# A hybrid attention and MLP layer on one core: latent token tiles loaded already turned, with the next tile's scaling put directly behind the queries' scaling

## What is computed

```python
def modulate(x, g, shift, scale):
    return rmsnorm(x, g) * (1.0 + scale) + shift

h_lat = modulate(x, g_attn[i], sh1, sc1)        # (1024, 1024)
h_ctx = modulate(ctx, g_attn[i], csh1, csc1)    # (256, 1024)
z = h @ w_in                                    # 1184 columns: cq, ckv, kr, qs, ks, vs
q_m = rmsnorm(rmsnorm(cq, g_q_a) @ w_uq)        # keys and values alike from ckv @ w_ukv
```

## Time and profile before

| | us |
|---|---|
| median of three executions | 1398.95 |
| the profiled execution's own time | 1399.78 |
| its span, first to last instruction | 1398.0 |
| token stage, steps 0 and 1 with the start, up to PE's `project(2, 0)` | 58.4 |
| step 2 | 25.8 |
| steps 3 to 8, each | 20.3 |
| step 9 and the last finishing, up to the first scores | 24.8 |
| attention, output projection and MLP | 1167 |

### The profile page before, as it was taken

The page is one execution under the profiler, slowest core; times in us unless marked ns, Lnnn a source line. Parts: engine busy times, 40 slices in busy tenths (PEclk is TensorE's granted clock), DMA queues, the critical chain, the costliest instruction groups (busy, mean ns, idle before and its releaser), DMA issues.

```text
span 1398.0 us, 18825 instructions
## 1 busy us (share of the span) xinstructions
PE 1357.5 (97%) x7262; PEld 1149.4 (82%) x7262; DVE 914.6 (65%) x1284; ACT 692.6 (50%) x1343; POOL 487.1 (35%) x321
## 2 busy tenths in 40 slices
PE   5899997999999999999999999999999999999999
PEld 1688987999899988988887888888888888888887
DVE  1878776777777877875774646547564654746463
ACT  2755655788778777972223424333332433333240
POOL 2766553121299992501102303132050323205010
PEclk8999998999999999999999999999999999999999
DMA  9555658433365646301123112121211212121013
GB/s 377 192 162 160 177 159 286 129 89 86 115 199 144 190 131 191 71 1 61 31 76 121 31 31 90 31 75 31 62 44 30 91 31 75 30 62 44 15 61 121
DMA packets 121576, 143.42 MB, mean 103 GB/s; under 512 B 8184, under 2 KB 103288, under 8 KB 118672
## 3 DMA queue, kind: packets, MB, share of 16 engines
q1 hardware_dynamic: 121232, 142.18, 32.6%
q0 software_dynamic: 256, 0.05, 0.0%
HBM read 108.38 MB, written 31.74 MB: 100 GB/s over the span
## 4 chain that ended last, share of the span: by engine, by line
PE 70%; DVE 11%; POOL 7%; ACT 6%; DMA 4%; issue 1%; SPq 1%; DVEq 0%; ACTq 0%; POOLq 0%
PE f_ps L2062 24%; PE f_ps L2331 19%; PE o_ps L1770 6%; PE a_ps L1422 4%; PE a_ps L1438 3%; PE f_ps L2347 3%; POOL l_wg L1349 3%; ACT s_pr L1519 3%; POOL l_gate L1351 3%; PE t_ps L956 2%; PE a_ps L1468 2%; DVE s_nmx L1604 2%; PE t_ps L945 1%; DMA t_wm<-in_w_mod 1%; DMA l_v<-scratch_v 1%
## 5 line engine op out<-in xcount | busy, mean ns | idle before, releaser
L2062 PE MATMUL f_ps<-h,f_w 128*128 128x512 f32 x1536 | 358.0, 389 | 0.4 <-DVE h L1836 0.2
L2062 PEld LDWEIGHTS f_ps<-h,f_w 128*128 128x128 f32 x1536 | 288.1, 188 | 60.7 <-DVE h L1836 0.7
L2261 DVE TENSOR_TENSOR mix<-mix,f_ps 128x512 f32<-128x512 f32 x196 | 128.7, 683 | 152.9 <-PE f_ps L2331 152.9
L2102 POOL TENSOR_TENSOR f_w<-f_w,f_g 128x1024 f32<-128x1024 f32 x30 | 77.0, 2590 | 390.2 <-DMA f_w<-in_w_mlp 342.7
L2139 ACT ACTIVATE f_a<-f_ps 128x512 f32<-128x512 f32 x64 | 38.2, 597 | 254.7 <-PE f_ps L2062 254.7
L2331 PE MATMUL f_ps<-f_bh,f_al 128*128 128x512 f32 x392 | 152.5, 389 | 0.0
L2331 PE MATMUL f_ps<-f_bh,f_ah 128*128 128x512 f32 x392 | 152.5, 389 | 0.0
L2331 PE MATMUL f_ps<-f_bl,f_ah 128*128 128x512 f32 x392 | 152.5, 389 | 0.0
L1618 DVE TENSOR_TENSOR l_pT<-a_ps,l_pT 128x512 fp32r<-128x512 f32 (+1 forms) x192 | 108.9, 594 | 54.0 <-ACT l_pT L1529 53.9
L1422 PE MATMUL a_ps<-l_k,l_q 96*128 96x512 f32 (+1 forms) x576 | 136.5, 366 | 1.6 <-DMA l_v<-scratch_v 1.1
L956 PE MATMUL t_ps<-w_in,t_h 128*128 128x416 f32 (+2 forms) x600 | 125.7, 355 | 0.3 <-DVE w_in L719 0.3
(11 more groups left out here) (223 smaller groups left out, 2425.1 us busy)
## 6 DMA issues: line engine op xcount, KB each, us to landing
l_wg<-in_w_mod SPq DMA_DIRECT2D x8, 2048.0 KB, 8.0
f_w1r<-in_w_mlp SPq DMA_DIRECT2D x32, 512.0 KB, 4.0
f_w<-in_w_mlp SPq DMA_DIRECT2D x16, 1024.0 KB, 5.0
t_wm<-in_w_mod SPq DMA_DIRECT2D x8, 1024.0 KB, 12.5
scratch_k<-t_kT SPq DMA_DIRECT2D x20, 384.0 KB, 3.7
l_k<-scratch_k SPq DMA_DIRECT2D x8, 960.0 KB, 10.6
scratch_q<-t_qT SPq DMA_DIRECT2D x16, 384.0 KB, 3.9
l_q<-scratch_q SPq DMA_DIRECT2D x8, 768.0 KB, 6.3
```

Source lines behind the costliest of these rows:

```text
L2062: last = nc.tensor.matmul(ps[:, b, :], w1[:, g % 2, w, k, :], h2[x][:, k, half * HB:(half + 1) * HB], start=(k == 0 and i == 0), stop=(k = ...
L2261: V.tensor_tensor(x, x, ps[:, bank_of(i, t), :].rearrange("p (k c) -> p k c", c=P), ALU.add).then_inc(added, 1)
```

## The change

- The host lays out the latent tokens a second time, turned: `x_cols`, per tile 128 rows of the model's width on the partitions, 8 times 128 tokens. SP loads these into `xT` (`load_xT`, 512 KB a tile); the untouched `x` is still loaded for the squares.
- `scale_x` of a latent tile becomes eight instructions of 128x128: each multiplies one block of `xT` by a column of `mods` (the scale, now a number for each partition) and by the inverse norms, which PE has turned into a PSUM bank by one transpose (the fill `x`, after the first part of `project(i, 1)`; for tile 2 after the seventh part of `project(1, 0)`).
- `add_shift` adds the shift from `mods`, repeated along the row. ACT takes the high part from `xT` in one instruction (`high_x`, between the splits of `q0` and `q1`), DVE the low part (`low_x`, behind the split of `q1`), in place of `xT`: the low part `lT` has the same memory as `xT`. `hT` and `lT` have two copies.
- The eight transposes of each latent tile go, with their splits; so do the four matmuls and the four copies for `scale_l` and `shift_l`. Four transposes of `mo` and one copy make `mods`.
- On DVE `scale_x` moves from behind `low_v` to directly behind `scale_q`, and `low_v` moves behind the split of `sk`.
- On SP `next_xT(i)`, which loads the turned tile i+2, comes behind the spill of tile i-1, and waits until tile i's projection is done; `next_xT(1)` stands behind the spill of tile 0's `k`.
- At the end of the MLP one semaphore counts the stores of the output in place of four.

```diff
+    xT = [room(f"t_xT{i}", [P, KC, P]) for i in range(2)]
+    low = Z.room("T", 9984)
+    lT = [low(f"t_l{i}", [P, KC, P], F32R) for i in range(2)]
...
+        ahead = [("x", i + 1)] if 0 < i < NT - 1 else []
+        if i < 2:
+            order += ahead + here + ([("x0", i + 1), ("x1", i + 1)] if i < 1 else [])
+        else:
+            order += ahead + ([("s", i - 1)] if lat(i - 1) else []) + [("sk", i - 1)] + here
+            order += [(k, i - 1) for k in (("k0", "k1", "q0", "q1") if lat(i - 1) else ("k0", "k1"))]
...
         def next_x(i):
-            sp.wait_ge(emptied, slot["x1", i] + 1)
+            sp.wait_ge(x_squared, i + 1)
+            if i < NCT:
+                sp.wait_ge(emptied, slot["x1", i] + 1)
             load_x(i + 2)
+
+        def next_xT(i):
+            sp.wait_ge(z_ready, z_at(i) + (3 if lat(i) else 1))
+            if i:
+                sp.wait_ge(xT_loaded, 16 * i)
+            load_xT(i + 2)
...
+        next_xT(0)
         next_x(1)
         spill_vs(0)
         spill_v(0)
         spill_vs(1)
         spill_rest(0)
+        next_xT(1)
         next_x(2)
         spill_v(1)
         spill_rest(1)
+        next_xT(2)
...
+        def high_x(t):
+            act.wait_ge(h_ready, t)
+            nc.scalar.activation(hT[t % 2][:, :, :], xT[t % 2][:, :, :], ACT.Copy).then_inc(h_hi, 1)
...
+            if lat(t):
+                dve.wait_ge(filled, slot["x", t] + 1)
+                dve.wait_ge(xT_loaded, 16 * (LATS(t) + 1))
+                for k in range(KC):
+                    x = xT[t % 2][:, k, :]
+                    ins = V.scalar_tensor_tensor(out=x, in0=x, scalar=mods[:, 8 + k:9 + k], in1=ps[:, slot["x", t] % 2, 0:P],
+                                                 op0=ALU.mult, op1=ALU.mult)
+                ins.then_inc(emptied, 1)
...
+        def low_x(t):
+            dve.wait_ge(h_hi, t - 1)
+            V.tensor_tensor(lT[t % 2][:, :, :], xT[t % 2][:, :, :], hT[t % 2][:, :, :].bitcast(F32), ALU.subtract).then_inc(h_lo, 1)
...
-                if i == 1:
-                    scale_x(2)
                 scale_s(i - 1)
                 if lat(i - 1):
                     scale_q(i - 1)
+                if i < NT - 1:
+                    scale_x(i + 1)
                 scale_k(i - 1)
-                low_v(i - 1)
-            if 1 < i < NT - 1:
-                scale_x(i + 1)
+                if i == 1 or i == NT:
+                    low_v(i - 1)
...
                 lo_fill("sk", i - 1)
+                if i < NT:
+                    low_v(i - 1)
...
-                project(i, 0, {1: ("sk", 0), 3: ("k0", 0), 5: ("k1", 0)} if i == NCT else {})
+                project(i, 0, {1: ("sk", 0), 3: ("k0", 0), 5: ("k1", 0)} if i == NCT else {6: ("x", 2)} if i == 1 else {})
...
+                ahead = {0: ("x", i + 1)} if i + 1 < NT else {}
...
-                if i + 1 < NT:
-                    fill("x0", i + 1)
-                    fill("x1", i + 1)
```

More of the change, by code:

```diff
@@ L177, in token_phase @@
     small = Z.small
+    mods = small("t_mods", [P, 16])
     stx = small("t_stx", [P, 2])
@@ L384, in sync @@
             spill(i - 1)
+            if i < NT - 2:
+                next_xT(i)
         sp.wait_ge(vs_spilled, 16 * NT)
@@ L644, in scalar @@
                     square_s(i)
-            if i == 0:
-                for n in range(4, 8):
-                    copy_spread(n)
             if i == 1:
@@ L665, in scalar @@
                     hi_fill("q0", i - 1)
-                    hi_fill("q1", i - 1)
+            if 1 < i < NT - 1:
+                high_x(i + 1)
+            if i > 1 and lat(i - 1):
+                hi_fill("q1", i - 1)
             if i < NT and not lat(i):
@@ L902, in vector @@
                 c_variances(i)
-            if i + 1 < NT:
-                lo_fill("x0", i + 1)
-                lo_fill("x1", i + 1)
+            if i == 0:
+                lo_fill("x0", 1)
+                lo_fill("x1", 1)
+            if 0 < i < NT - 1:
+                low_x(i + 1)
             if i == 0:
@@ L1009, in tensor @@
         fill("x1", 0)
+        for c in range(4):
+            ins = nc.tensor.transpose(ps[:, MB, c * P:c * P + P], mo[:, c * P:c * P + P], ident[:, :])
+        ins.then_inc(spread, 1)
         def project_first():
@@ L1016, in project_first @@
                     for a in range(2):
-                        MM(ps[:, ZB, 0:NA], hT[a][:, k, :], w_in[0][:, k, 0:NA], start=(k == 0 and a == 0), stop=False)
+                        MM(ps[:, ZB, 0:NA], (hT, lT)[a][0][:, k, :], w_in[0][:, k, 0:NA], start=(k == 0 and a == 0), stop=False)
             pe.wait_ge(first_low, 1)
@@ L1027, in tensor @@
             if 0 < i < NT:
[L1028 to L1032 removed]
+                if lat(i):
+                    pe.wait_ge(h_lo, i - 1)
+                else:
+                    pe.wait_ge(emptied, slot["x1", i] + 1)
+                project(i, 0, {1: ("sk", 0), 3: ("k0", 0), 5: ("k1", 0)} if i == NCT else {6: ("x", 2)} if i == 1 else {})
             if i < NT and not lat(i):
                 fill("c", i)
[L1035 to L1036 removed]
                 if i == 0:
+                    fill("x0", 1)
+                    fill("x1", 1)
                     pe.wait_ge(w_lo, JOBS.index("kv"))
[L1039 removed]
                 pe.wait_ge(emptied, slot["c", i] + 1)
@@ L1984, in mlp_phase @@
     added = sem("f_added")
-    stored = [sem(f"f_stored{i}") for i in range(4)]
+    stored = sem("f_stored")
     w1_dram = A["w_mlp1"][0].rearrange("(k p) (f c) -> f p k c", p=P, c=P)
@@ L2093, in sync @@
             sp.dma_start(out[0, row * P:(row + 1) * P, dh * HB:(dh + 1) * HB],
-                         fin[:, 2 * row + dh, :]).then_inc(stored[n % 4], 16)
-        for i in range(4):
-            sp.wait_ge(stored[i], 16 * 4)
+                         fin[:, 2 * row + dh, :]).then_inc(stored, 16)
+        sp.wait_ge(stored, 16 * len(LAST_OUT))
     def gpsimd():
```

94 lines of the change are left out of this document (47 added, 47 removed).

## The result

The changed kernel took 1402.5 us (median of 16 runs) against 1399.4 us for the kernel before in the same jobs: a ratio of 1.0019, with a 95% interval of 1.0012 to 1.0027, or 2.7 us slower. One of the 16 runs took 1925.7 us at a mean granted clock of 0.655; the ratio leaves it out, and without it the median is 1401.7 us. In a second job the ratio was 1.0032 (1.0020 to 1.0044). Forecast were 1397.0 us and a range that ended at 1401.3, so the time lies outside it, and on the other side of the kernel before.

The account below looks back on a forecast made before the run. PE was taken to bound steps 3 to 8, with DVE close behind, while in step 2 PE waits for DVE. Terms -4.6, +2.4 and +0.2 gave -2.0 us, so 1397.0 us, range 1394.3 to 1401.3.

Parts of the forecast that it names:

- Steps 3 to 8: Six middle latent steps, PE-bound: dropping eight transposes saves 0.81 us each; counted as -4.6 us, bounds 2.8 and 5.4.
- the cover of SP's later load: Middle steps: the load, issued at a step's end and needed nearly 5 us into the next, leaves 2 to 3 us.
- The last mark of the list: Sign of a wrong forecast: ACT waiting for the spill of vs, queued behind one more load; no size given.
- `low_v` "at no cost": Middle steps on DVE: `low_v`, moved ahead of `low_vs`, fits into a wait that exists anyway, at no cost.
- The prices of the operations: Middle steps: DVE's eight scalings 2.25 us, keys' scaling 0.7, `low_x` 1.2; ACT's large copy about 1.05.
- Rival 4: Middle steps give little: eight pieces take 2.8 us or more, PE waits for `sk`; 1399; chance 0.12 together with Rival 5.
- Rival 5: Middle steps: POOL's query rotation waits for `low_x`, up to 1.2 us a step, sum unchanged; chance 0.12 together with Rival 4.
- Steps 0 to 2: Step 2 and all ahead of it: 2.4 us later, mainly through tile 3's late load; bounds 0.6 and 5.5.
- The matmuls and copies saved at the start end in the same waits: Start of the token stage: savings vanish in waits for POOL's add and tile 2's landing; counted nothing, at best 0.5 us.
- The 0.2 ahead of the attention's first loads: End of the latent steps: later spills ahead of the attention's first loads cost 0.2 us.
- Rival 2: Step 2: tile 3 lands before DVE reaches it, so the kernel is faster, -4.1 us, 1394.9; chance 0.25.
- Rival 3: Step 2: PE's wait ahead of `k1` lowers the clock and the split of `c` comes later; +3, 1402; chance 0.11.

Follow-up runs that it names:

- the three moves and the rows: Changed kernel with t_vs spill, tile 3 load and later turned-tile loads issued earlier, plus unread matmuls in PE's waits of steps 0 and 1; 0.9949 and 0.9967 of before.
- e15: Changed kernel with `low_v` back in its old place, directly behind the keys' scaling in every step; 1.0045 of the time before.
- e2: Changed kernel with the load of turned tile 3 issued ahead of the spills of tile 0 instead of behind them; 1.0014 of the time before.

## Why the prediction was wrong

- **Steps 3 to 8, the term that failed.** -4.6 was counted, with -2.8 as the bound; the two profiles have -1.5 and -1.4 (B without step 9). The step that failed is the cover of SP's later load: "a landing of 5.3 from an issue some 3 us ahead of that step's start leaves 2 to 3 us." In step 4 the load was issued 1.3 us ahead of the step's start (105.68 for 106.97), and DVE reached the tile 5.0 us into the step (111.95); the landings took what the summary of the load's line says:

```profile
DMA to landing us min/median/max: 5.6/6.0/7.1
```

  So the median landing left 0.3 us and not 2 to 3, and in two of the six steps the tile was late, by 0.41 and 1.06. The 5.3 came from step 2, the 3 us from no row at all. I had not laid the step's transfers on one time line. With the three moves and the rows the six steps are 4.2 and 4.3 us shorter than before, near what this term had promised.
- **The last mark of the list.** "ACT waiting for the spill of vs" was named as what would make the forecast wrong, and was given no price and no chance: the sum held it at nothing. It came, 6.1 us in four steps, and in two of these it is the only late transfer; it should have been a rival.
- **`low_v` "at no cost".** On DVE that was right: in its old place PE waits 0.33 us more a step (e15). But the prediction did not follow the DMA that waits for `low_v`: the spill of t_vm went 4.3 us later into the step, and SP keeps in order what stands behind it. 1.9 of these come back with the old place, the rest belongs to the scaling ahead; what they cost is not shown.
- **The prices of the operations held.** Eight L728 took 2.16 (2.25 taken), `low_x` 1.21 (1.2), the keys' scaling 0.75 (0.7), ACT's large copy 1.05 (1.05). A step that goes well gains 0.65, not 0.81: PE now waits 0.3 ahead of the fill of `q` for the split of `k`, where it waited 0.12. Rival 4 did not come: PE did not wait for `sk` in steps where the tile had landed. Rival 5 came in part and cost nothing: `low_x` was not held up, but POOL's first rotation of the queries, which starts beside it, took 1.75 for 1.30 in every middle step. For the eight, the Trainium skill's "VectorE: DVE Perf Modes", section on the TRN2 errata, gave by estimate 2.1 with its table and 2.3 with its other figure; the trace, at 2.16, lies nearer the table. The rows are PE's, DVE's and POOL's of step 3, and POOL's of the kernel before:

```profile
100.67 0.66 PE L995 MATMUL t_ps<-ident,t_qn 128*128 128x128 f32 x4 [0.31 <-DVE t_kT L784]
...
103.73 1.21 DVE L738 TENSOR_TENSOR t_l<-t_xT,t_h 128x1024 fp32r<-128x1024 f32 x1
...
104.36 1.75 POOL L424 TENSOR_TENSOR t_ros<-t_z,t_tab 128x512 f32<-128x512 f32 x1 [3.82 <-ACT t_z L581]
```

```profile
100.96 1.30 POOL L400 TENSOR_TENSOR t_ros<-t_z,t_tab 128x512 f32<-128x512 f32 x1 [3.03 <-ACT t_z L552]
```

- **Steps 0 to 2.** +2.4 was counted and +2.7 came, as a mean of +1.6 and +3.8. Less the 1.7 us by which the first profile's `project_first` is late, the load of tile 3 was issued at 66.9 (67.3), DVE had it at 72.6 (72.6), and PE's `k1` came at 80.5 (81.0). The sum held partly by luck: the low clock at 46 us, over 1 us, was not in it. "The matmuls and copies saved at the start end in the same waits" was right about the waits and silent about what the matmuls did for the clock. The 0.2 ahead of the attention's first loads was 0.5.
- **Rival 2**, with tile 3 in time, is what e2 made: 0.7 to 2.5 us by the ratios, and no faster kernel, since the middle steps stayed uneven.
- **Rival 3** had a chance of 0.11 for a slower kernel, through the clock in step 2. Its 1402 is near the measured time by luck. The kernel is slower, partly through the clock, but in steps 0 and 1; in step 2 it was low from 70 to 73 us, as before, and at full behind the wait of 1.93 us ahead of `k1`.
